# A projection group moved ahead of the gates of the last token chunk, and three exponentials moved ahead of a copy, in a two-layer mixer block

## The chip, the cores and the metric

The kernel runs on one core of one Trainium2 chip. The metric is device time in microseconds (us) of one execution. The kernel before takes 1721.24 us (median of 3 runs, 1720.3 to 1721.43). The trace is of one further execution of 1724.45 us, whose span is 1722.7 us.

## The reference, cut to what matters

The reference computes two layers over 256 context tokens and 1024 latent tokens of width 1024, all in float32. Layer 0 (gated linear attention and neighbourhood attention) ends in an output projection, a residual sum and a layer norm. Layer 1 begins with an mLSTM of four heads, whose queries, keys, values and gates are products of the normed and modulated tokens:

```python
qm, km, vm, _, gates = parts[:5]
q = heads(qm, ML_HEADS)
k = heads(km, ML_HEADS) * (ML_DQK ** -0.5)
v = heads(vm, ML_HEADS)
gp = gates.reshape(gates.shape[:2] + (2, 2, ML_HEADS)).astype(F32) + ml_gate_b.astype(F32)
...
x = layer_norm(ALPHA * x + gate[:, None] * y, ln_g[l], ln_b[l])
```

The mLSTM scan goes over chunks of 64 tokens in both directions. Its weights are exponentials of running sums and running maxima of the gates. Nothing of this is changed.

## The kernel before

**How the work is laid out.** Activations lie transposed, features on the 128 partitions, tokens along the free axis: `hT` (the input of the products) and `yT` each hold 8 tiles of 1280 tokens. A projection of 128 output features is a group of 8 matmuls per token chunk, one for each 128 input features, accumulated in one PSUM bank and then copied out. The token chunks are 0 to 256 (context), 256 to 768 and 768 to 1280. Values are made the other way round, tokens on the partitions, in groups of 256 tokens. The four mLSTM heads are handled as two pairs, called `("ml", 0, ...)` and `("ml", 1, ...)`. The two pairs' scans follow each other.

**Who does what in the stretch of the change.** `make_schedule` (L392) writes one list of steps by hand. Every engine walks through the same list in this order and issues only its own part of each step, so a step that waits holds up everything behind it on that engine, and on no other. The steps are:

- `("mm", kind, dest, t0, n, ...)`, in four parts, is one projection group. TensorE does its matmuls (L977). Its first part waits for the weight tile to have been loaded (L982) and for the PSUM bank to be free. At the fourth part ScalarE copies the bank out (L1737).
- `("scale", ...)` and `("next", ...)` end a layer norm. In `scale` VectorE multiplies (L1658) and ScalarE writes the modulated tokens to `hT` (L1908). In `next` VectorE makes the normed tokens in `yT` (L1676), and the DMA queue of SyncE (SP) stores them to HBM in pairs, after a wait for VectorE (L896 to L902). The last tokens (1024 to 1280) are normed last; this is norm 3.
- `gates` and `gates_sum` are the products for the gates of one chunk. `gates` (L1035) waits until the norms of its tokens are complete. ScalarE copies the result to a stage, TensorE sums it, and ScalarE writes two gate rows to `yT` (L1709, L1714).
- `("rows", 0)` (tokens 0 to 768) and `("rows", 1)` (768 to 1280) are the running sums and maxima over the gate rows, on VectorE (L1588). Each needs an exponential and a logarithm of ScalarE near its start (L1872, keys `rows_abs` and `rows_log`).
- `("rows_exp",)` is three exponentials on ScalarE over 64 x 1280 elements (L1879). They wait for the last VectorE operation of `rows`.
- `("rows_turn", t, ...)` transposes the rows of two token tiles on TensorE (L1282); the first one waits for the three exponentials (key `rows_act`). The scans follow.

**Pacing.** `pace` (L195) puts the steps of the norms and the products into one order. It counts planned microseconds of the norm steps, and it puts in products until their planned sum (tokens / 300 for each part of a projection) has caught up. What is left of the products comes behind the last norm step. The list called `ready` holds products of layer 1 that need only tokens 0 to 768; `rest` holds what needs the last tokens.

**Weights.** There are five tiles for weights (`WBUFS`), used in turn in the order of `PLAN`, which is the order in which the schedule first names each weight. SP issues the loads in its own walk through the schedule. It does so at the last product that uses a weight, and then loads up to four places further on:

```python
if s[0] == "mm" and LAST_PRODUCT.get(s[1]) == s:
    load_weights(WEIGHT_AT[s[1]] + WBUFS + (s[1][2:] == ("v0",)))
```

In `PLAN` the weights here stand as (out, 0, 7, 3), (ml, 0, q), (ml, 0, k), (ml, 0, v0), (ml, 0, v1), (ml, 1, q), (ml, 1, k). The last product with (ml, 0, q) is its group for tokens 768 to 1280, which stands in `rest`, behind `("rows", 0)`. So (ml, 1, q) is loaded when SP comes to that place. The tile that it is loaded into was last read by (out, 0, 7, 3), the last output projection.

Of the kernel before, what the change touches and what calls it, by code (L numbers as in the profile page):

```python
# [62 lines left out]
CHUNKS_LAT = CHUNKS_ALL[1:]  # L63
# [175 lines left out]
def project(kind, dest, chunks):  # L239

    out = []
    for t0, n in chunks:
        bank, stage = Slot(), Slot()
        out += [("mm", kind, dest, t0, n, bank, stage, part) for part in range(4)]
        if dest in ("rq", "kk") and t0 >= CTX:
            out.append(("rope", kind, dest, t0, n, Slot(), stage))
    if dest == "v":
        out += [("vgather", kind[1], g, Slot()) for g in range(-(-VG // 4))]
    return out
# [8 lines left out]
def values(group, j):  # L258

    return project((group, j, "v0"), "vt", [(t0, 2 * P) for t0 in range(0, T, 2 * P)])  # L260
# [40 lines left out]
def scans(l, fills):  # L301


    steps = [dict(l=l, p=p, i=i, t=(scan_order(0)[i], scan_order(1)[i]), wanted=(l == 0 or i >= CT))
             for p in range(2) for i in range(NT)]
    for q in steps:
        q["second"] = q["t"][0] in scan_order(1)[:q["i"]]
        assert q["second"] == (q["t"][1] in scan_order(0)[:q["i"]])
        q["d"] = (0, 1) if q["t"][0] < q["t"][1] else (1, 0)
        q["t"] = tuple(sorted(q["t"]))  # L310
    out, main = [], []
    for x in range(2 * NT + 3):
        if x in (NT, NT + 3):
            out += interleave(main, fills[x > NT])
            main = []
        now, one, two, three = (steps[x - y] if 0 <= x - y < 2 * NT else None for y in range(4))
        turned = three and three["second"] and three["wanted"]
        if turned:
            main.append(("lin_square", three))
        if two:  # L320
            main += [("lin_chunk", two, 0), ("lin_inside", two)]
        if one:
            main.append(("lin_attend", one))
        main.append(("gap",))
        if now:
            main.append(("lin_scale", now))
        if turned:
            main += [("lin_norm", three), ("lin_turn", three, Slot())]
        if two:
            main += [("lin_chunk", two, 1), ("lin_out", two)]  # L330
        if now:
            main.append(("lin_mul", now))
        main.append(("gap",))
    return out + interleave(main, fills[2])


def ada(l, tiles):

    out = []
    for x in range(0, len(tiles), 4):  # L340
        fs = tuple(tiles[x:x + 4])
        out += [("ada", l, fs, Slot()), ("ada_turn", l, fs, Slot())]
    return out


def ada_first(x):
    return (x, x + 1, 8 + x, 9 + x)
# [19 lines left out]
def qkv(group, j, chunks_q=CHUNKS_ALL):  # L367
    out = []
    for w in ("q", "k", "v") if group == "na" else ("q", "k"):
        out += project((group, j, w), w, chunks_q if w == "q" else CHUNKS_ALL)  # L370
    return out if group == "na" else out + values(group, j)


def between(products, extra):

    ends = [i + 1 for i, s in enumerate(products)
            if s[0] != "mm" and (i + 1 == len(products) or products[i + 1][0] == "mm")
            or s[0] == "mm" and s[7] == 3 and (i + 1 == len(products) or products[i + 1][0] == "mm")]
    out, at, used = [], 0, 0
    for n, e in enumerate(ends):  # L380
        out += products[at:e]
        at = e
        while used < (n + 1) * len(extra) // len(ends):
            out.append(extra[used])
            used += 1
    return out
# [5 lines left out]
def make_schedule():  # L392

    s, depth = [("setup",)], 0
    for x in range(0, KT, 2):
        s += [("ada", 0, ada_first(x), None), ("ada_turn", 0, ada_first(x), None), ("modulate", x), ("modulate", x + 1)]
        while depth < (x + 1 if x + 2 < KT else KT):
            s.append(("early", depth))
            depth += 1
    s += [("early_copy",)] + project(("lr",), "lr", CHUNKS_ALL)  # L400
    s += between(values("gla", 0), [("gate0", t) for t in GATE_ORDER])
    na = qkv("na", 0)
    na_v = [x for x in na if x[1] == ("na", 0, "v")]
    s += scans(0, [qkv("gla", 1), na_v, between([x for x in na if x not in na_v], ada(0, range(16, 24)))])
    gates = [project(("gate", 0, f), "gate", [c]) for f in range(8) for c in CHUNKS_ALL]
    fills = [between(qkv("na", j + 1), ada(1, range(8 * j, 8 * j + 8))) for j in range(3)] + [sum(gates[9:18], [])]
    s += attention(0, fills, [sum(gates[3 * j:3 * j + 3], []) for j in range(3)])
    s += sum(gates[18:], [])
    s += [("banks", 6)] + out_projection(0, 0, NORMS[:1])
    parts = [out_projection(0, ci, NORMS[ci:ci + 1]) for ci in range(1, 4)]  # L410
    s += [("blend",)] + pace(normalise(0, 0), parts[0])

    gates = [[(kind, t0, n, Slot(), stage) for kind in ("gates", "gates_sum")]
             for (t0, n), stage in ((c, Slot()) for c in CHUNKS_ALL)]
    q, k, v = project(("ml", 0, "q"), "q", CHUNKS_LAT), project(("ml", 0, "k"), "k", CHUNKS_ALL), values("ml", 0)
    ready = [gates[0][0], gates[1][0]] + q[:4] + [gates[0][1], gates[1][1]] + k[:8] + v[:12]
    rest = [gates[2][0], q[4], gates[2][1]] + q[5:] + [("rows", 1)] + k[8:] + v[12:] + [("rows_exp",)]
    s += pace(middle_norms(), parts[1] + parts[2] + ready) + [("rows", 0)] + rest
    q = project(("ml", 1, "q"), "q", CHUNKS_LAT)
    turns = [("rows_turn", t, Slot()) for t in range(0, NT, 2)]  # L420
    s += q[:4] + sum(([turn, x] for turn, x in zip(turns, q[4:])), []) + turns[4:]
    s += [("banks", 2)]
    fill = project(("ml", 1, "k"), "k", CHUNKS_ALL)
    fill += values("ml", 1)
    gates = [project(("gate", 1, f), "gate", [c]) for f in range(8) for c in CHUNKS_LAT]
    rq = [project(("sw", j, "q"), "rq", CHUNKS_LAT) for j in range(4)]
    s += scans(1, [fill + sum(gates[8:12], []), project(("sw", 0, "k"), "kk", CHUNKS_ALL) + gates[12],
                   project(("sw", 0, "v"), "vv", CHUNKS_ALL) + rq[0] + sum(gates[13:] + gates[:4], [])])
    s += attention(1, [rq[1], rq[2], rq[3], gates[7]], gates[4:7])
    s += [("banks", 6)] + out_projection(1, 1, NORMS[1:2])  # L430
    parts = [out_projection(1, ci, NORMS[ci:ci + 1]) for ci in range(2, 4)]
    s += pace(last_norms(), parts[0] + parts[1])
    s += [("column_sum", 1, 3)] + norm(1, 3)

    banks, stages, out = {}, {}, []
    single, newest, width = None, {}, 2
    for st in s:
        st = list(st)
        if st[0] == "one_bank":
            single = st[1] if st[2] else None  # L440
            if st[2]:
                BEFORE_ATT[st[1]] = newest[1]
            else:
                newest[1] = ("att", st[1])
            continue
        if st[0] == "banks":
            width = st[1]
            for b in range(2, 6):
                newest.pop(b, None)
                BANK_TURN.pop(b, None)  # L450
            continue
        at = {"mm": 5, "rope": 5, "ada": 3, "ada_turn": 3, "lin_turn": 2, "rows_turn": 2, "vgather": 3, "gates": 3, "gates_sum": 3}.get(st[0])
        if at is not None and st[at] is not None:
            fresh = st[at] not in banks
            st[at] = banks.setdefault(st[at], len(banks))
            if fresh:
                u = st[at]
                b = 0 if single is not None else min(range(width), key=lambda k: BANK_TURN.get(k, -1))
                BANK_OF[u], FORMER[u] = b, newest.get(b)
                newest[b], BANK_TURN[b] = u, u  # L460
        if st[0] in ("mm", "rope"):
            staged = st[2] == "gate" or (st[2] in ("rq", "kk") and st[3] >= CTX)
            st[6] = stages.setdefault(st[6], len(stages)) if staged else None
        if st[0] in ("gates", "gates_sum"):
            st[4] = stages.setdefault(st[4], len(stages))
        out.append(tuple(st))
    return out
# [1662 lines left out]
```

How the kernel before makes its waits and increments, by code:

```python
        def wait_bank(pe, u):  # L683
            former = FORMER[u]
            if former is None:
                return
            if isinstance(former, tuple):
                pe.wait_ge(*at(("softmax_dve", ("att", former[1], 3, N_UNITS[former[1]] - 1))))
            else:
                pe.wait_ge(*at(("proj_free", former)))
# [143 lines left out]
            def load_weights(upto):  # L835
                while sent[0] < min(upto, len(PLAN)):
                    n = sent[0]
                    if n >= WBUFS:
                        sp.wait_ge(*at(("weight_used", n - WBUFS)))
                    sp.dma_start(weights[:, n % WBUFS, :, :], a["weights"][n]).then_inc(
                        *up(f"weight_loaded{n % WBUFS}", ("weight", n), by=16))
                    sent[0] += 1
# [1 line left out]
            def load_residuals(upto, layer):  # L844
                while sent[1] < min(upto, len(RESID)) and RESID[sent[1]][1][1] == layer:
                    (_, l, f, _), t0, n, i = *RESID[sent[1]][1:2], *RESID[sent[1]][3:5], sent[1]
                    if i >= 4:
                        sp.wait_ge(*at(("resid_used", i - 4)))
                    if f == 0 and t0 == (CTX if l else 0):
                        sp.wait_ge(*at(("att_pe", l, 3)))
                        sp.wait_ge(*at(("y_turned", l, 7)))
                        if l:
                            for ci in range(1, 4):
                                sp.wait_ge(*at(("first_spill", ci)))
                                sp.wait_ge(*at(("spill", ci)))
```

## Time and profile before

| | |
|---|---|
| median of 3 runs | 1721.24 us |
| profiled execution | 1724.45 us, span 1722.7 us |
| TensorE (PE) busy | 1620.0 us, 94% |
| VectorE (DVE) busy | 672.9 us, 39% |
| ScalarE (ACT) busy | 548.4 us, 32% |
| GpSimd (POOL) busy | 36.6 us, 2% |
| mean granted TensorE clock | 0.983 of full speed |

Times of day in the rows are microseconds from the start of the span. L12 is line 12 of the kernel. One float32 matmul of 512 columns appears as two records, so a projection group of 8 matmuls counts x16. Most operations of ScalarE are issued through one helper and carry its line, L1701; they are told apart by the tiles that they write. The granted clock is 1.00 at 2.4 GHz and 0.50 at 1.2 GHz.

### The profile page before, as it was taken

The page shows a single profiled execution, that of the slowest core. Times are in us where ns is not written, and L with a number is a line of the kernel's source. Part 1 is how long each engine was busy: PE and PEld are TensorE (multiplying, and loading weights), DVE is VectorE, ACT ScalarE, POOL GpSimd, SP SyncE. Part 2 cuts the span into 40 slices and gives each one's busy share as a digit, 9 for nine tenths or more (in the row PEclk, how much of TensorE's full clock was granted, in tenths as well). Part 3 has the DMA queues.
Part 4 walks back from the last instruction along what each step waited for, and adds up shares of the span by engine and source line. Part 5 has one row for each costly group of instructions (what it writes and reads, how often), then busy time and mean ns, then how long its engine had stood idle before and what let it go on. Part 6 is the DMA issues. An engine that isn't in the chain of part 4 may idle for free.

```text
span 1722.7 us, 25991 instructions
## 1 busy us (share of the span) xinstructions
PE 1620.0 (94%) x10106; PEld 1023.8 (59%) x10106; DVE 672.9 (39%) x1537; ACT 548.4 (32%) x1253; POOL 36.6 (2%) x108
## 2 busy tenths in 40 slices
PE   6999999899999999888999989999899899999996
PEld 4676876556556556554746755675474355555475
DVE  2123443423313214321254735135345255555256
ACT  0242141323423324432121432124213355555024
POOL 0000000000000000000000000000000001111000
PEclk9999999899999999999999999999999899999999
DMA  9100021111223023000454511000001000000344
GB/s 381 58 25 25 2 99 63 62 62 59 89 74 123 16 70 123 25 13 14 149 181 153 178 45 49 25 26 26 13 2 50 13 13 14 25 13 14 128 140 160
DMA packets 41145, 120.63 MB, mean 70 GB/s; under 512 B 4288, under 2 KB 14784, under 8 KB 39744
## 3 DMA queue, kind: packets, MB, share of 16 engines
q1 hardware_dynamic: 41024, 118.97, 19.8%
q8 instruction: 82, 1.34, 0.3%
q14 instruction: 39, 0.32, 0.1%
HBM read 109.52 MB, written 9.44 MB: 69 GB/s over the span
## 4 chain that ended last, share of the span: by engine, by line
PE 77%; issue 16%; DVE 3%; ACT 3%; DMA 1%; POOL 0%; SPq 0%; DVEq 0%; ACTq 0%; POOLq 0%
PE proj L1012 22%; PE mixed L1012 15%; PE scores L1012 6%; PE proj L996 5%; PE mixed L996 4%; PE mixed L1132 3%; PE turned L1118 3%; PE scores L1230 2%; PE scores L1098 2%; PE scores L1258 2%; PE scores L1101 1%; ACT vstage L1701 1%; PE turned L1269 1%; PE mixed L957 1%; PE turned L957 1%
## 5 line engine op out<-in xcount | busy, mean ns | idle before, releaser
L1012 PE MATMUL proj<-hT,weights 128*128 128x512 f32 (+1 forms) x1264 | 513.5, 553 | 10.4 <-DVE yT L1380 3.6
L1012 PEld LDWEIGHTS proj<-hT,weights 128*128 128x128 f32 x1264 | 235.1, 194 | 215.8 <-issue 204.7
L1012 PE MATMUL mixed<-hT,weights 128*128 128x512 f32 (+1 forms) x336 | 144.5, 573 | 0.8 <-ACT pair L1701 0.8
L1012 PE MATMUL mixed<-yT,weights 128*128 128x256 f32 (+1 forms) x432 | 123.0, 442 | 0.0
L1701 ACT ACTIVATE work<-work,stat 128x640 f32<-128x640 f32 (+8 forms) x144 | 108.8, 755 | 42.8 <-DVE stat L1439 39.0
L1538 DVE SCALAR_TENSOR_TENSOR work<-work,turned 128x128 f32<-128x128 f32 (+1 forms) x152 | 53.1, 349 | 143.4 <-PE turned L1269 140.2
L1701 ACT ACTIVATE work<-turned 128x512 f32<-128x512 f32 (+2 forms) x136 | 72.7, 534 | 109.6 <-PE turned L1114 98.3
L1118 PEld LDWEIGHTS turned<-consts,work 128*128 128x128 f32 (+4 forms) x656 | 74.8, 140 | 54.6 <-issue 34.0
L1118 PE MATMUL turned<-consts,work 128*128 128x128 f32 (+4 forms) x656 | 99.8, 279 | 7.8 <-ACT work L1701 7.8
L1012 PEld LDWEIGHTS mixed<-yT,weights 128*128 128x128 f32 x432 | 82.1, 190 | 38.9 <-issue 31.1
L1012 PEld LDWEIGHTS mixed<-hT,weights 128*128 128x128 f32 x336 | 62.2, 191 | 62.3 <-issue 60.1
L1456 DVE COPY work<-turned 128x512 f32<-128x512 f32 (+1 forms) x72 | 46.6, 647 | 120.2 <-PE turned L1118 114.1
L1012 PE MATMUL scores<-yT,weights 128*128 128x256 f32 (+1 forms) x320 | 91.2, 443 | 0.0
L1701 ACT ACTIVATE work<-mixed 128x256 f32<-128x256 f32 x80 | 30.7, 383 | 176.7 <-PE mixed L1170 172.1
L996 PE MATMUL proj<-weights,hT 128*128 128x256 f32 x352 | 80.2, 382 | 0.0
L1012 PEld LDWEIGHTS scores<-yT,weights 128*128 128x128 f32 x320 | 60.8, 190 | 29.2 <-issue 23.4
L1701 ACT ACTIVATE vstage<-proj 128x512 f32<-128x512 f32 (+1 forms) x41 | 23.0, 560 | 164.9 <-PE proj L1012 142.6
L996 PEld LDWEIGHTS proj<-weights,hT 128*128 128x128 f32 x352 | 66.0, 190 | 11.5 <-issue 2.8
L1380 DVE TENSOR_TENSOR yT<-yT,proj 128x512 f32<-128x512 f32 (+1 forms) x28 | 17.4, 621 | 139.5 <-ACT vstage L1701 139.4
L996 PE MATMUL mixed<-weights,hT 128*128 128x256 f32 x288 | 65.1, 382 | 0.0
L996 PEld LDWEIGHTS mixed<-weights,hT 128*128 128x128 f32 x288 | 54.1, 190 | 9.7 <-issue 2.6
L1701 ACT ACTIVATE pair<-proj 128x512 f32<-128x512 f32 (+1 forms) x30 | 16.0, 533 | 123.0 <-PE proj L1012 100.8
(252 smaller groups left out, 2124.3 us busy)
## 6 DMA issues: line engine op xcount, KB each, us to landing
weights<-in_weights SPq DMA_DIRECT2D x138, 512.0 KB, 3.7
tables<-in_bias SPq DMA_DIRECT2D x8, 1281.0 KB, 7.2
hT<-in_xT SPq DMA_DIRECT2D x8, 640.0 KB, 16.0
yT<-in_weights SPq DMA_DIRECT2D x8, 512.0 KB, 8.4
work<-in_xT SPq DMA_DIRECT2D x24, 128.0 KB, 3.4
x1T<-yT SPq DMA_DIRECT2D x12, 256.0 KB, 2.2
work<-in_weights SPq DMA_DIRECT2D x4, 512.0 KB, 17.0
pair<-in_weights SPq DMA_DIRECT2D x4, 512.0 KB, 17.8
```

Source lines behind the costliest of these rows:

```text
L957: last = nc.tensor.matmul(early_bank(w, t0), weights[:, n, k, :], hT[:, k, t0:t0 + m], start=(k == 0 and (w == "q" or t0 > 0)), stop=(k == ...
L996: last = nc.tensor.matmul(PJ[BANK_OF[u]][:, 2 * x * P:2 * (x + 1) * P], tokens, weights[:, lo:hi + 1:hi - lo, k, :], start=(k == 0), stop= ...
L1012: last = nc.tensor.matmul(PJ[BANK_OF[u]][:, 0:n], weights[:, w % WBUFS, k, :], src[:, k, t0:t0 + n], start=(k == 0), stop=(k == KT - 1))
L1098: last = nc.tensor.matmul(to[:, lat_lo:lat_lo + unit.nk], q, unit_keys(keys, unit), start=True, stop=True)
L1118: last = nc.tensor.transpose(to[0:w, :], prob[uid[3] % 2][hh][:, o:o + w], ident)
L1132: last = nc.tensor.matmul(OV[rows, 0:P], vals[0:w, place, rows], prob_t[i % 2][0:w, at_col:at_col + P], start=(x == 0), stop=(x == nch - 1))
L1230: last = nc.tensor.matmul(out_of(l, h, x)[r, :], buf(q, "at")[r, o:o + CHUNK], pv(lin_slot(l, p))[r, t, h, 0:VW if l else P], start=False, ...
L1258: last = nc.tensor.matmul(out_of(l, h, x)[half * CHUNK:(half + 1) * CHUNK, :], buf(q, "qin")[r, o:o + CHUNK], state[d][r, 0:vw], start=(n ...
L1380: link(V.tensor_tensor(y, y, ps, ALU.mult), ("proj_free", u))
L1456: link(V.tensor_copy(prob_t[i % 2][:, 512 * g:512 * g + n], TP[1][:, 0:n]), ("pt", uid, g))
L1538: link(V.scalar_tensor_tensor(out=state[d][:, 0:vw], in0=state[d][:, 0:vw], scalar=decays(q)[:, o:o + 1], in1=TP[half][:, P:P + vw], op0=A ...
L1701: link(nc.scalar.activation(out, in_, func, **kw), *keys)
```

## The change

The group of the second pair's queries for tokens 256 to 768 (`others[:4]`) is appended to `ready`. It stood behind `rest` before, just ahead of the first `rows_turn`. It now stands ahead of the last chunk's `gates`. `("rows_exp",)` stood behind all of the value groups of the first pair. It now stands ahead of the last of them (tokens 1024 to 1280). No instruction is added or removed.

```diff
     ready = [gates[0][0], gates[1][0]] + q[:4] + [gates[0][1], gates[1][1]] + k[:8] + v[:12]
-    rest = [gates[2][0], q[4], gates[2][1]] + q[5:] + [("rows", 1)] + k[8:] + v[12:] + [("rows_exp",)]
+    others = project(("ml", 1, "q"), "q", CHUNKS_LAT)
+    ready += others[:4]
+    rest = [gates[2][0], q[4], gates[2][1]] + q[5:] + [("rows", 1)] + k[8:] + v[12:16] + [("rows_exp",)] + v[16:]
     s += pace(middle_norms(), parts[1] + parts[2] + ready) + [("rows", 0)] + rest
-    q = project(("ml", 1, "q"), "q", CHUNKS_LAT)
     turns = [("rows_turn", t, Slot()) for t in range(0, NT, 2)]
-    s += q[:4] + sum(([turn, x] for turn, x in zip(turns, q[4:])), []) + turns[4:]
+    s += sum(([turn, x] for turn, x in zip(turns, others[4:])), []) + turns[4:]
     s += [("banks", 2)]
```

## Rows read from the trace of the kernel before

**Rows 1.** The page, chain that ended last: shares of the span by engine.

```profile
PE 77%; issue 16%; DVE 3%; ACT 3%; DMA 1%; POOL 0%; SPq 0%; DVEq 0%; ACTq 0%; POOLq 0%
```

**Rows 2.** Windows: length, busy us (x instructions) by engine, clock, DMA share, GB/s.

```profile
1020.00:1026.00 6.00, 1.23 (x6) 0.75 (x4) 4.60 (x12) 4.44 (x8) 0.00 (x0) 0.97 0.14 49
1026.00:1040.00 14.00, 12.75 (x36) 4.87 (x37) 10.57 (x15) 4.99 (x8) 0.00 (x0) 0.77 0.28 92
```

**Rows 3.** Chain of waits, 1015 to 1080 us: start, length, what.

```profile
1017.78 3.47 PE proj L996 x16
...
1027.25 3.64 PE scores L1043 x16
...
1033.61 0.86 PE mixed L1051 x2
1034.47 5.15 PE scores L1012 x12
1039.62 6.87 PE mixed L1012 x16
...
1053.39 6.91 PE proj L996 x32
1060.30 6.87 PE scores L1012 x16
1067.16 0.52 PE scores L1288 x6
```

**Rows 4.** Timeline, TensorE: start, length, engine, line, operation [idle before, releaser].

```profile
979.05 1.92 PE L1043 MATMUL mixed<-hT,tables 128*32 128x512 f32 x16
```

**Rows 5.** Timeline of SP's DMA queue, 1027 to 1029 us.

```profile
1027.54 0.36 SPq L900 DMA_DIRECT2D x1T<-yT  x1
1027.95 0.47 SPq L840 DMA_DIRECT2D weights<-in_weights  x1
```

**Rows 6.** Line L840, the weight loads: that at 1027.95; then all from 950 to 1100.

```profile
DMA to landing us min/median/max: 3.7/3.7/3.7
...
DMA to landing us min/median/max: 3.4/3.7/6.5
```

**Rows 7.** Timeline, ScalarE, 1000 to 1100 us.

```profile
1028.92 0.84 ACT L1701 ACTIVATE yT<-yT 64x768 f32<-64x768 f32 x1 [1.92 <-DVE yT L1600]
1029.80 0.93 ACT L1701 ACTIVATE yT<-yT,cols 64x768 f32<-64x768 f32 x1
...
1039.71 0.60 ACT L1701 ACTIVATE pair<-scores 128x512 f32<-128x512 f32 x1 [3.76 <-PE scores L1012]
...
1061.02 1.27 ACT L1701 ACTIVATE work<-work 64x1280 f32<-64x1280 f32 x1
1062.33 2.57 ACT L1701 ACTIVATE yT<-yT 64x1280 f32<-64x1280 f32 x2
```

**Rows 8.** Timeline, VectorE, 1000 to 1100 us.

```profile
1030.84 0.95 DVE L1603 SCALAR_TENSOR_TENSOR yT<-yT 64x768 f32<-64x768 f32 x1 [2.01 <-ACT yT L1701]
...
1039.07 0.68 DVE L1600 SCALAR_TENSOR_TENSOR yT<-yT 64x512 f32<-64x512 f32 x1
1041.83 0.68 DVE L1603 SCALAR_TENSOR_TENSOR yT<-yT 64x512 f32<-64x512 f32 x1 [2.08 <-ACT yT L1701]
...
1055.02 3.00 DVE L1634 TENSOR_TENSOR yT<-yT,work 32x1280 f32<-32x1280 f32 x2
```

**Rows 9.** Windows of 1 us, columns as in Rows 2.

```profile
1025.00:1026.00 1.00, 0.00 (x0) 0.00 (x0) 0.58 (x2) 0.93 (x3) 0.00 (x0) 0.82 0.50 168
...
1032.00:1033.00 1.00, 1.00 (x3) 0.37 (x2) 0.83 (x3) 0.00 (x0) 0.00 (x0) 0.77 0.00 0
```

**Rows 10.** Timeline, TensorE, 1330 to 1375 us, after stalls elsewhere.

```profile
1330.20 1.96 PE L1012 MATMUL proj<-hT,weights 128*128 128x512 f32 x4 [1.62 <-DVE yT L1374]
...
1342.70 5.37 PE L1012 MATMUL proj<-hT,weights 128*128 128x512 f32 x8 [2.07 <-DVE yT L1380]
...
1349.66 3.70 PE L1012 MATMUL proj<-hT,weights 128*128 128x512 f32 x8
1357.03 1.12 PE L1279 MATMUL mixed<-consts,work 128*128 128x128 f32 x4 [3.67 <-DVE work L1586]
1358.71 9.52 PE L1012 MATMUL proj<-hT,weights 128*128 128x512 f32 x16
```

## Prediction

> **What bounds the kernel now.** I read the chain of waits first. It runs through TensorE for 77% of the span [rows 1], so what counts is when TensorE stands still, at which clock it runs, and what it waits for. Windows come next. In the stretch of the change TensorE is busy 1.23 of 6 us, and the clock is 0.77 of full over the 14 us behind that [rows 2]. The chain then shows the pieces: the value group of `ready` ends at 1017.78 + 3.47 = 1021.25; the gates of the last chunk start at 1027.25, when norm 3 has filled `hT`; so 6.0 us stand idle [rows 3]. The clock fell to 0.50 (1.2 GHz) at about 1025.64 (0.82 in a window of 1 us is 0.64 us at 1.00 and 0.36 at 0.50) and came back at about 1032.46 [rows 9]. TensorE worked 1032.46 - 1027.25 = 5.2 us at half speed and lost 2.6 us by it. A check: the gates took 3.64 us, against 1.92 for the same form at full clock [rows 3, 4]. The hole thus costs 6.0 + 2.6 = 8.6 us. From 1034.47 TensorE is unbroken up to the first `rows_turn` at 1067.16 [rows 3]. Last I read the queues of the other engines, because a moved step moves in each of them.
>
> **The change, part by part.**
>
> *The moved group itself.* It is 6.87 us of matmuls at full clock (the group at 1060.30) [rows 3]. It needs only tokens that are ready, so on its own it would fill the hole of 6.0 us. Its PSUM bank is no matter: by the turn order its former user is the gate sum of tokens 256 to 768, long copied out.
>
> *Its weight.* It needs the tile (ml, 1, q). SP issues that load at the last product with (ml, 0, q), which stays in `rest`. On SP's walk all stores of norm 3 lie ahead of it, and each waits for VectorE. The trace shows just that: the last store goes out at 1027.54, and the next entry of the queue is this load, at 1027.95 [rows 5]. The tile has long been free, for the last output projection was over before the gates at 979.05 [rows 4]; it is SP's order that holds the load. The change moves the use ahead of the hole, and not the load. The load takes 3.7 us to land, 3.4 to 6.5 for all loads around [rows 6]. The chain to `hT` and the stores (norm 3 on ScalarE and VectorE) waits for nothing that is moved, so the load still goes out at 1027.95 and lands at 1031.65 (1031.35 to 1034.45). There is no way round for TensorE: the gates, ready at 1027.25, are queued behind the waiting group. The idle time grows from 6.0 to 1031.65 - 1021.25 = 10.4 us.
>
> The Trainium skill, "DMA: Bandwidth & Descriptors", section "Rules for kernel authors", says to issue a DMA early, compute, and wait on its semaphore late. This change puts the wait some 39 us earlier (1060.30 to 1021.25) with the issue where it was, so the rule speaks against it. The same page's fixed cost of about 2.0 us plus bytes over 436 GB/s (section "Anatomy of one DMA", which is for another issuing path) gives an estimate of 3.2 us for 512 KB; the trace has 3.7, and by the page the time would be 0.5 us less.
>
> *The clock.* Between 1021.25 and 1031.65 it falls as before, and TensorE again works a while at half speed after it resumes. The nearest row is 5.2 us, a loss of 2.6. The bounds come from other stalls: behind one of 2.07 us eight records took 5.37 where they take 3.70, a loss of 1.7; behind one of 3.67 us a group of 16 records took 9.52 where 6.87 is usual in the chain, and the transposes ahead of it 1.12, half of it lost: about 2.6 + 0.6 = 3.2 [rows 3, 10]. I take 2.6, as now, with 1.7 and 3.2 as ends. So the moved group ends at 1031.65 + 6.87 + 2.6 = 1041.12.
>
> *What is queued behind it on ScalarE.* `pace` decides where its copy stands. At the `rstd` of norm 3 the planned products are at 85.92 and the norms at 86.2, and each part adds 512 / 300 = 1.71. So the four parts fall behind `rstd`, `scale` 2, `scale` 5 and `next` 0. ScalarE's copy belongs to the fourth part, thus behind all eight `scale` steps: `hT` is not held up. But it stands ahead of `("rows", 0)`. ScalarE's exponential and logarithm, which ran from 1028.92 to 1030.73 [rows 7], now wait for the copy (0.60, as the one at 1039.71): 1041.15 + 0.60 + 0.03 + 1.81 = 1043.59. VectorE waits for them, and its first L1603 moves from 1030.84 [rows 8] to 1043.7, by 12.86 us.
>
> *The rows chain.* From there to the second L1600, which ended at 1039.75, nothing changes but the shift. The second pair of exponential and logarithm lost 0.56 us behind the copy at 1039.71 [rows 7, 8]; now VectorE is the late one and this goes. So the chain ends at 1058.02 - 0.56 + 12.86 = 1070.32 (1058.02 is the end of L1634 [rows 8]).
>
> *The moved exponentials.* They took 1061.02 to 1064.90, 3.88 us, and started behind the copy of the last values, 3.0 us after VectorE was done [rows 7, 8]. Ahead of that copy they start with VectorE: 1070.4 + 3.88 = 1074.28. The copy goes behind them. The scan needs it only with its values, so it costs nothing; if it did, 0.6 us.
>
> *TensorE in the meantime.* After 1041.12: gates 1.92, the first part of the queries 1.72 (a quarter of 6.87), the gate sum 0.86, which needs the stage at about 1044.25 and finds it there; then 5.15 + 6.87 + 2 x 6.91 [rows 3, 4]. That is 1071.5. The first `rows_turn` waits for the exponentials until 1074.35: a new stall of 2.9 us, where before the moved group covered them. `rows_turn` thus comes 1074.35 - 1067.16 = 7.2 us later than now.
>
> *The second fall of the clock.* A stall of 1.62 us left the records at 1.96 for four, the full speed; those of 2.07 and 3.67 us did not [rows 10]. A stall of 2.9 us lies between the two latter, so I take the smaller loss, 1.7 us (0 to 3.2). The Trainium skill, "TensorE: Matmul & The Clock Gate", section "What's actually happening", says that the point of change depends on a phase that runs free of the kernel. By it the loss here may also be nothing, which is the second rival.
>
> *Sum.* 7.2 + 1.7 = 8.9 us. Behind the turns the same work follows at the same distance, and all engines are shifted alike, so nothing gives it back. The terms are of the execution of 1724.45 us; its stretch is taken as that of the runs, and 1721.24 + 8.9 = 1730.2 us.
>
> **The rivals.**
>
> *Faster: the weight is there in time.* If the load were out by about 1017.6, the moved group would run from 1021.25 to 1028.12 at full clock. The gates would start 0.9 us later than now, with no loss by the clock. The sum would end at 1028.12 + 1.92 + 1.72 + 0.86 = 1032.62, and the last values at 1058.5. The rows chain would end at 1058.02 - 0.56 = 1057.46 and the exponentials at 1061.4, so the turn comes 5.7 us earlier: -5.7, or -4.0 if the clock falls in that stall too: 1717.2, or 1715.5. For it: the tile is free since before 979.05. Against it: SP's order [rows 5], in which no load stands ahead of the stores. It decides at the issue time of this one load: each us later than 1017.6 is an us lost. 0.05.
>
> *The clock stays up in the new stall.* Then 1721.24 + 7.2 = 1728.4. For it: a stall of 1.62 us cost nothing. Against: 2.07 us did. 0.25.
>
> *Only the wait for the weight counts.* If the rows were ready by the time TensorE comes, the turn would be at 1071.5: +4.3, 1725.5. It needs ScalarE not to hold the rows behind the copy; its one queue says otherwise. 0.06.
>
> *A slower load.* The stores just ahead of it could hold it up. At 6.5 us [rows 6] both chains slip by 2.8: 1733.0. For it: one of the loads around took as long; against: this very one, behind the same stores, took 3.7. 0.06.
>
> **How the numbers follow.** The forecast, slower by 8.9, has 0.58. Range: 1726.5 to 1733.5. It takes in the second rival, the bounds 1.7 and 3.2 on the first clock loss, and most of the fourth; it leaves out the faster case and most of the third. Differences within 0.2% (3.4 us) can't be told from none. Faster by more: 0.05. Within: 0.03, from the third rival with a short clock loss. Slower by more: 0.92.
>
> **What would show it.** Right: TensorE's longest wait in the stretch is one for a weight DMA of about 10.4 us, and behind it come the queries, not the gates; SP issues the load at about 1027.95; ScalarE's first exponential over 64 x 768 starts at about 1041.8; VectorE waits some 15 us in L1603 of part 0; and the first `rows_turn` stands idle about 3 us for ScalarE, at 1074. Wrong: a weight load ahead of the last store; or a `rows_turn` that doesn't wait, which would refute the rows chain as the second limit.

## The result, and the profile after

The changed kernel takes 1732.61 us (median of 4 runs, 1732.13 to 1734.23) against 1721.12 us for the kernel before (median of 4, 1720.3 to 1721.43). The ratio is 1.0071, with a 95% interval of 1.0056 to 1.0086: 0.7% slower. Measured again (e11) it was 1730.68 against 1720.9 us, ratio 1.0060 (1.0046 to 1.0073). The profiled execution took 1732.67 us, with a span of 1730.9 us.

The page after, busy time by engine and the chain's shares (the row of before is in [rows 1]):

```profile
PE 1620.8 (94%) x10106; PEld 1022.4 (59%) x10106; DVE 672.9 (39%) x1537; ACT 549.4 (32%) x1253; POOL 36.8 (2%) x108
PE 75%; issue 16%; DVE 4%; ACT 3%; DMA 1%; POOL 0%; SPq 0%; DVEq 0%; ACTq 0%; POOLq 0%
```

The page barely shows the loss. TensorE's timeline does (start, length, operation, in brackets the idle time before and what ended it):

```profile
1014.34 3.62 PE L997 MATMUL proj<-weights,hT 128*128 128x256 f32 x16
1028.39 9.90 PE L1013 MATMUL scores<-hT,weights 128*128 128x512 f32 x16 [10.44 <-DMA weights<-in_weights]
1038.23 1.92 PE L1044 MATMUL scores<-hT,tables 128*32 128x512 f32 x16
...
1061.68 7.07 PE L997 MATMUL scores<-weights,hT 128*128 128x256 f32 x32
1071.63 0.90 PE L1289 MATMUL scores<-consts,yT 64*128 64x64 f32 x6 [2.87 <-ACT yT L1702]
1072.46 3.21 PE L1013 MATMUL mixed<-hT,weights 128*128 128x512 f32 x4
1075.60 0.59 PE L1289 MATMUL mixed<-consts,yT 64*128 64x64 f32 x6
1076.12 1.98 PE L1013 MATMUL mixed<-hT,weights 128*128 128x512 f32 x4
```

The hole of 6.0 us ahead of the gates [rows 2, 3] is now one of 10.44 us ahead of the moved queries, and what ends it is the weight. The gates behind them run at full speed, 1.92 us as in [rows 4]. TensorE then stands idle for 2.87 us ahead of the first `rows_turn`, and the piece behind it takes 3.21 us where the next one of its kind takes 1.98. SP's queue answers to [rows 5]; the chain of waits gives the landing:

```profile
1020.47 4.16 SPq L901 DMA_DIRECT2D x1T<-yT  x4
1024.67 0.47 SPq L841 DMA_DIRECT2D weights<-in_weights  x1
```

```profile
1024.67 3.68 DMA weights<-in_weights
1028.39 9.92 PE scores L1013 x16
1038.38 0.61 ACT pair L1702
1039.01 0.85 ACT yT L1702
```

The load still goes out behind the four stores and lands 3.7 us later. (This trace is 3.28 us ahead of that of before when the last value group ends, 1017.96 against 1021.24, so its 1024.67 is the 1027.95 of [rows 5].) The chain then shows the second limit: behind the queries comes ScalarE's copy, and only behind it the exponential of `rows`. ScalarE's own timeline and then VectorE's, for [rows 7, 8]:

```profile
1038.38 0.60 ACT L1702 ACTIVATE pair<-scores 128x512 f32<-128x512 f32 x1 [14.66 <-PE scores L1013]
1039.01 0.84 ACT L1702 ACTIVATE yT<-yT 64x768 f32<-64x768 f32 x1
...
1067.70 1.27 ACT L1702 ACTIVATE work<-work 64x1280 f32<-64x1280 f32 x1 [5.15 <-DVE yT L1635]
1069.00 2.57 ACT L1702 ACTIVATE yT<-yT 64x1280 f32<-64x1280 f32 x2
```

```profile
1040.94 0.95 DVE L1604 SCALAR_TENSOR_TENSOR yT<-yT 64x768 f32<-64x768 f32 x1 [15.39 <-ACT yT L1702]
...
1064.61 3.00 DVE L1635 TENSOR_TENSOR yT<-yT,work 32x1280 f32<-32x1280 f32 x2
```

The clock in windows (columns as in [rows 2]), for [rows 9]: at half for the whole 5.6 us after TensorE resumes, and again for 3.4 us behind the second stall.

```profile
1028.40:1034.00 5.60, 5.60 (x7) 2.50 (x8) 0.00 (x0) 0.00 (x0) 0.00 (x0) 0.50 0.00 0
1071.60:1075.00 3.40, 3.37 (x9) 1.89 (x10) 0.00 (x0) 0.81 (x2) 0.00 (x0) 0.51 0.40 163
```

**Three stretches.** The time varies by some us between executions of one kernel, so all traces are cut in three for comparison. The *start* goes to the end of the last value group ahead of the hole. The *stretch* goes from there to the start of the last `rows_turn`. The *rest* follows. "Clock" is half of TensorE's busy time at 1.2 GHz, summed over windows of 0.25 us; "net" is the stretch less its clock. Time against before is the difference of the medians of runs taken together. The lengths of the stretch are good to 0.2 us, all in the same direction, so their differences are good to 0.1.

| kernel | stretch | its clock | net | rest | its clock | time against before |
|---|---|---|---|---|---|---|
| before | 55.7 | 2.6 | 53.1 | 645.9 | 9.3 | |
| changed | 65.1 | 4.5 | 60.6 | 648.0 | 11.3 | +11.5 |
| changed again (e11) | 65.6 | 5.2 | 60.4 | 646.1 | 9.5 | +9.8 |
| e1, early load | 51.7 | 1.7 | 50.0 | 646.2 | 9.6 | -0.4 |
| e8, e1 again | 51.7 | 1.7 | 50.0 | 646.1 | 9.6 | -2.2 |
| e2, queries only | 66.7 | 4.3 | 62.4 | 644.6 | 8.1 | +13.2 |
| e3, exponentials only | 55.8 | 2.7 | 53.1 | 645.8 | 9.3 | +0.3 |
| e4, rows first | 61.8 | 2.1 | 59.7 | 646.3 | 9.7 | +9.6 |
| e5, load after first store | 62.3 | 5.2 | 57.0 | 646.2 | 9.5 | +8.6 |
| e6, early load in before | 54.9 | 1.7 | 53.2 | 644.3 | 7.8 | -0.1 |
| e7, early load and cover | 45.9 | 0.0 | 45.9 | 647.4 | 11.1 | -9.7 |
| e9, late load and cover | 59.1 | 2.5 | 56.7 | 646.3 | 9.8 | +2.7 |
| e10, e7 with old exponentials | 45.9 | 0.0 | 45.9 | 645.0 | 8.3 | -10.5 |

From before to changed: the net stretch grew by 7.5 (10.44 - 6.02 = 4.4 at the DMA, 2.9 at `rows_turn`, and 0.2 that no row names), its clock by 1.9, and the rest by 2.1, of which 2.0 is clock. That is 11.5 us, as much as the medians differ by. The same sum with the second trace of the changed kernel (e11) gives 10.1 against a measured 9.8. The match to a tenth is luck in part, since these sums leave out the start: its end lies anywhere from 1016.1 to 1021.2 us in the 13 traces, though the products up to there are the same. The spans differ by 8.2 only, because the profiled execution of before took 3.3 us more in the start; it was 3.2 us above its median.

### The profile page after: what moved, and what is told of

It reads as the page before. It is cut to its first block, busy times and chain, and to the rows that moved or that the text cites. A ratio compares the mean times of both kernels' runs of the same rounds, so it can differ in the third digit from the quotient of the medians.

```text
span 1730.9 us, 25991 instructions
## 1 busy us (share of the span) xinstructions
PE 1620.8 (94%) x10106; PEld 1022.4 (59%) x10106; DVE 672.9 (39%) x1537; ACT 549.4 (32%) x1253; POOL 36.8 (2%) x108
## 4 chain that ended last, share of the span: by engine, by line
PE 75%; issue 16%; DVE 4%; ACT 3%; DMA 1%; POOL 0%; SPq 0%; DVEq 0%; ACTq 0%; POOLq 0%
PE proj L1013 22%; PE mixed L1013 15%; PE scores L1013 6%; PE proj L997 4%; PE mixed L997 3%; PE mixed L1133 3%; PE turned L1119 3%; PE scores L1231 2%; PE scores L1099 2%; PE scores L1259 2%; PE scores L1102 1%; ACT vstage L1702 1%; PE turned L1270 1%; PE mixed L958 1%; PE turned L958 1%
## 5 line engine op out<-in xcount | busy, mean ns | idle before, releaser
L1013 PE MATMUL proj<-hT,weights 128*128 128x512 f32 (+1 forms) x1264 | 512.4, 552 | 10.4 <-DVE yT L1381 3.6
L1013 PE MATMUL mixed<-hT,weights 128*128 128x512 f32 (+1 forms) x352 | 155.0, 585 | 0.8 <-ACT pair L1702 0.8
L1539 DVE SCALAR_TENSOR_TENSOR work<-work,turned 128x128 f32<-128x128 f32 (+1 forms) x152 | 53.1, 349 | 142.4 <-PE turned L1270 139.2
L1013 PEld LDWEIGHTS mixed<-hT,weights 128*128 128x128 f32 x352 | 66.3, 195 | 68.4 <-issue 66.2
L997 PE MATMUL mixed<-weights,hT 128*128 128x256 f32 x256 | 58.0, 382 | 0.0
L997 PEld LDWEIGHTS mixed<-weights,hT 128*128 128x128 f32 x256 | 48.0, 190 | 8.5 <-issue 2.1
```

Of the source, the lines that this page charges most:

```text
L997: last = nc.tensor.matmul(PJ[BANK_OF[u]][:, 2 * x * P:2 * (x + 1) * P], tokens, weights[:, lo:hi + 1:hi - lo, k, :], start=(k == 0), stop= ...
L1013: last = nc.tensor.matmul(PJ[BANK_OF[u]][:, 0:n], weights[:, w % WBUFS, k, :], src[:, k, t0:t0 + n], start=(k == 0), stop=(k == KT - 1))
L1539: link(V.scalar_tensor_tensor(out=state[d][:, 0:vw], in0=state[d][:, 0:vw], scalar=decays(q)[:, o:o + 1], in1=TP[half][:, P:P + vw], op0=A ...
```

## The experiments

**e1: the load in time.** The changed kernel, with SP's load ahead of the stores of norm 3:

```diff
+                if s[0] == "next" and s[1:] == (3, 1):
+                    load_weights(WEIGHT_AT[("ml", 1, "q")] + 1)
                 if s[0] == "next" and s[2] % 2:
```

> The changed kernel, with one load moved in SP's walk: the tile (ml, 1, q) is loaded ahead of the first store of norm 3, where its buffer has long been free. Theory (the late load is the cause): TensorE no longer waits for a weight DMA, the moved group fills the hole, ScalarE's first exponential over 64 x 768 starts near its old place, and the first rows_turn still waits about 2.9 us for the moved exponentials. Against before: -4.0 if the clock falls in that stall, -5.7 if not, so 1715.5 to 1717.2 us; against the changed kernel -15 to -17. Rival (the order of the products costs by itself, through the rows chain or ScalarE's queue): the wait for the DMA goes but the time stays above that of before, 1722 or more.

Measured: 1719.31 us (11 runs, 1715.85 to 1720.99) against 1719.68, ratio 0.9994 (0.9985 to 1.0004). The timeline of TensorE:

```profile
1014.34 3.62 PE L999 MATMUL proj<-weights,hT 128*128 128x256 f32 x16
1017.79 7.03 PE L1015 MATMUL scores<-hT,weights 128*128 128x512 f32 x16
1024.75 1.92 PE L1046 MATMUL scores<-hT,tables 128*32 128x512 f32 x16
...
1058.26 0.58 PE L1291 MATMUL scores<-consts,yT 64*128 64x64 f32 x6 [2.98 <-ACT yT L1704]
1058.77 2.66 PE L1015 MATMUL mixed<-hT,weights 128*128 128x512 f32 x4
```

SP's queue and VectorE's timeline in the same trace:

```profile
987.13 0.49 SPq L841 DMA_DIRECT2D weights<-in_weights  x1
```

```profile
1027.56 0.95 DVE L1606 SCALAR_TENSOR_TENSOR yT<-yT 64x768 f32<-64x768 f32 x1 [2.01 <-ACT yT L1704]
```

The load goes out 30.7 us ahead of its use. The hole and its low clock are gone, and nothing else was altered: the late load is the cause of the first loss. VectorE waits 2.01 us in part 0 of `rows`, as in before [rows 8], and not 15.39. The stall at `rows_turn` is there all the same, 2.98 us, so it doesn't need a late copy on ScalarE: the moved group no longer stands ahead of the turns to cover it. The stretch is 4.0 us shorter than in before, as expected. The time is not: it is 0.4 us below before, where 4.0 to 5.7 were expected.

**e8: the same kernel again.**

> The same kernel as e1_early_load, for a second trace and more timed runs. There the trace had the turn 5.7 us earlier than in before, and a low clock of 3.4 us behind the new stall, which makes -4.0; the median was only 0.4 us below before. Theory A (the loss of clock behind the new stall is 1.7 in some executions and 3.4 in others, and later falls come with it): in this trace the first rows_turn again waits 3.0 us and comes 40.2 us after the end of the last value group of the first stage; what differs from run to run is the time at the low clock only; median 1 to 4 us below before. Theory B (something else in the later stages is longer): the stretch behind the turns is over 658 us with no more low clock in it.

Measured: 1717.47 us (11 runs, 1710.92 to 1721.62) against 1719.67, ratio 0.9987 (0.9975 to 0.9998). The stretch is again 51.7 us, and the rest 646.1 with 9.6 of clock, so theory B holds in neither trace. The two medians lie 0.4 and 2.2 us below before; the stretch says 4.0. The 1.8 to 3.6 us between them aren't in either trace, and both traced executions (1717.49 and 1715.94 us) were faster than the median of their kernel, by 1.8 and 1.5 us. The mean granted clock of the 22 timed runs is no higher than that of before (0.984 for both), although in the traces the stretch spends 3.4 us at the low clock against 6.8 in before, which would be 0.001 more. That hints at the clock at other stalls. It isn't shown: the other timed runs have no trace, and theory B isn't excluded for them.

**e5: a dose.** The load behind the first of the four stores (`(3, 3)` in place of `(3, 1)` in the edit of e1).

> A dose of the delay: the changed kernel with the load of (ml, 1, q) behind the first of the four stores of norm 3, not behind the last. In the changed kernel's trace the first store goes out at 1020.5 and the load at 1024.7, so the load goes out about 3.8 us earlier. Theory (TensorE and, through ScalarE's queue, the rows chain both hang on the landing): the wait for the DMA is about 6.6 in place of 10.4 us, the first rows_turn comes 3.8 us earlier, and the time is 3.8 us below the changed kernel's, give or take 1.7 of the clock: about 12.3 - 0.8 - 3.8 = 7.5 us above before, 1727 us. Rival (a fixed harm of having the group there): about as slow as the changed kernel, above 1730.

Measured: 1728.28 us (5 runs, 1727.76 to 1728.71) against 1719.67, ratio 1.0055 (1.0041 to 1.0069). SP's queue and TensorE:

```profile
1020.77 0.36 SPq L903 DMA_DIRECT2D x1T<-yT  x1
1021.17 0.47 SPq L841 DMA_DIRECT2D weights<-in_weights  x1
1022.04 2.89 SPq L903 DMA_DIRECT2D x1T<-yT  x3
```

```profile
1025.24 9.27 PE L1015 MATMUL scores<-hT,weights 128*128 128x512 f32 x16 [6.98 <-DMA weights<-in_weights]
...
1067.84 0.90 PE L1291 MATMUL scores<-consts,yT 64*128 64x64 f32 x6 [2.87 <-ACT yT L1704]
1068.67 3.78 PE L1015 MATMUL mixed<-hT,weights 128*128 128x512 f32 x4
```

The wait is 3.46 us shorter (3.8 were expected; this load took 4.0 us to land), the net stretch 3.6, and the stall at `rows_turn` is the same to 0.01 us. So both engines' chains hang on the landing. The whole stretch fell by 2.8 only, since the clock took 3.0 behind `rows_turn` here, and 1.6 in the changed kernel's first trace; against its second (e11), with 3.0 as here, it fell by 3.3. The time, 8.6 us above before where about 7.5 was expected, is 1.2 to 2.9 us below the changed kernel's +9.8 and +11.5. Timed runs don't show more of where the rest went.

**e6: the early load in the kernel before.** The edit of e1 on before.

> A control: the kernel before with only the load of (ml, 1, q) moved ahead of the stores of norm 3. Theory: in the kernel before the tile is used at about 1060 us and lands at 1031 us, so an earlier load changes nothing: the same time as before within 0.1%. Rival (the early load helps or harms by itself, beside the stores of norm 2 or by freeing the queue behind the stores of norm 3): a difference of over 2 us.

Measured: 1719.57 us (11 runs) against 1719.67, ratio 1.0001 (0.9993 to 1.001). The load by itself does nothing.

**e2 and e3: each part alone.** e2 leaves the exponentials where they were; e3 moves them alone.

```diff
-    rest = ... + v[12:16] + [("rows_exp",)] + v[16:]
+    rest = ... + v[12:] + [("rows_exp",)]
```

> The first part of the change alone: the query group ahead of the gates, the three exponentials behind the copy of the last values, as in the kernel before. Theory: the exponentials start 0.6 us behind the end of the last values instead of as soon as VectorE is done; the copy ends about 2 us after that point, so rows_turn waits about 4.5 us in place of 2.9 and the time is 1.5 to 2 us above the changed kernel: about 1734.3 us. Rival (the moved exponentials are part of the harm): below the changed kernel, 1731 or less.

> The second part of the change alone, on the kernel before: only the three exponentials ahead of the copy of the last values. Theory: they start at VectorE's end, 3.0 us earlier, but rows_turn comes behind the query group anyway, so nothing changes: 1721.2 us within 0.1%. Rival (the delayed copy of the last values or the earlier exponentials count by themselves): a difference of over 2 us either way.

Measured: e2 1732.88 us (6 runs, 1729.23 to 1735.48) against 1719.68, ratio 1.0072 (1.0056 to 1.0088); e3 1719.96 us (12 runs), ratio 1.0000 (0.999 to 1.0011). In e2's trace `rows_turn` waits 1.8 us longer than in the changed kernel, by the net stretch (62.4 against 60.6):

```profile
1071.08 0.90 PE L1289 MATMUL scores<-consts,yT 64*128 64x64 f32 x6 [4.65 <-ACT yT L1702]
```

e2 is no faster than the changed kernel, and e3 is as fast as before: the queries do all the harm. The moved exponentials give back 1.8 us of it in the traces (the medians don't resolve that), and alone they are worth nothing.

**e4: rows ahead of the copy.** The moved group one step later, behind `("rows", 0)`:

```diff
-    s += pace(middle_norms(), parts[1] + parts[2] + ready) + [("rows", 0)] + rest
+    s += pace(middle_norms(), parts[1] + parts[2] + ready) + [("rows", 0)] + others[:4] + rest
```

> The changed kernel with the moved group one step later: behind rows 0, still ahead of the last chunk's gates. TensorE's order is the same and the load is as late, so it waits 10.4 us as before; but ScalarE's exponential and logarithm for rows 0 now stand ahead of the copy of the moved group. Theory (two limits, the second being ScalarE's queue behind the copy): VectorE's wait in rows 0 goes back to about 2 us, the first rows_turn doesn't wait, and of the 11.4 us lost only the part of the longer DMA wait remains: 10.4 - 6.0 = 4.4, so about 1725.5 us (1724 to 1728 with the clock's phase). Rival (only the DMA wait and the clock count, the stall at rows_turn is a by-product): no gain over the changed kernel, 1731 to 1734.

Measured: 1729.29 us (5 runs, 1728.07 to 1730.7) against 1719.68, ratio 1.0053 (1.0038 to 1.0069). The expectation, 1724 to 1728, failed, and the rival's 1731 to 1734 as well. VectorE's timeline has the reason:

```profile
1027.90 0.95 DVE L1603 SCALAR_TENSOR_TENSOR yT<-yT 64x768 f32<-64x768 f32 x1 [2.01 <-ACT yT L1701]
...
1044.26 0.68 DVE L1600 SCALAR_TENSOR_TENSOR yT<-yT 64x512 f32<-64x512 f32 x1 [8.16 <-ACT yT L1701]
1050.04 0.68 DVE L1603 SCALAR_TENSOR_TENSOR yT<-yT 64x512 f32<-64x512 f32 x1 [5.11 <-ACT yT L1701]
```

The wait in part 0 went back to 2.0 us, as meant. But part 1 needs the gate rows of the last chunk, which come late because TensorE is late, and its exponential then stands behind the copy of the next query group. The 13.4 us won in part 0 were mostly lost again in part 1, where VectorE waits 8.2 + 5.1 us against 1.6 in the changed kernel, and `rows_turn` still waited 1.73 us. The rows hang on TensorE's delay at two places, not at one.

**e9: the second limit taken away.** The late load kept; the other half of the queries as one group ahead of the row transposes:

```diff
-    s += sum(([turn, x] for turn, x in zip(turns, others[4:])), []) + turns[4:]
+    s += others[4:] + turns
```

> The changed kernel with the load as late as it is there, but the other half of the moved queries as one group ahead of the five row transposes. It takes away the second limit alone (the rows chain behind ScalarE's copy, which reached rows_turn 2.9 us late), since 6.9 us of products now cover it. Theory (two limits in series): TensorE still waits 10.4 us for the DMA, and the first rows_turn doesn't wait. From the end of the last stalled products: 3.2 us less for the stall, 1.7 for the clock and 0.8 to 1 for the unsplit parts, so 5 to 6 us below the changed kernel, about 1726 us. Rival (the stall at rows_turn is not a cost of its own): within 2 us of the changed kernel.

Measured: 1723.62 us (11 runs, 1721.27 to 1727.74) against 1720.9, ratio 1.0015 (1.0006 to 1.0024), and 7.1 us below the changed kernel measured beside it (e11), where 5 to 6 were expected:

```profile
1028.04 9.58 PE L1013 MATMUL scores<-hT,weights 128*128 128x512 f32 x16 [10.57 <-DMA weights<-in_weights]
...
1067.91 7.03 PE L1013 MATMUL scores<-hT,weights 128*128 128x512 f32 x16
1074.88 1.34 PE L1289 MATMUL mixed<-consts,yT 64*128 64x64 f32 x18
```

There is no wait at `rows_turn`. So the stall there, with its clock and the split parts, was worth 6 us (65.1 to 59.1 in the traces; 6.5 from e11's 65.6).

**e7 and e10: both mended.** The edits of e1 and e9 together; e10 also puts the exponentials back.

> The changed kernel with the early load of e1_early_load and, beside it, the second half of the moved queries (tokens 768 to 1280) as one whole group ahead of the five row transposes, which then come back to back. Theory: the group (6.9 us) covers the 3.0 us in which rows_turn waited for the exponentials in e1_early_load, so TensorE doesn't stand still from the last values to the scans, and the clock has no cause to fall there. From the chain: the stall of 3.0, the clock's 1.7 and about 0.8 of start-up between the split parts go, 5.5 us less than e1_early_load; 8.5 to 9.4 us below before if all of it shows in the time, 1710 to 1711.5 us. Rival (the clock's low stretches come back at other stalls, so that a stall taken away gives less than its length): 3 to 6 us below before, 1713.5 to 1716.5.

> e7_cover with the three exponentials behind the copy of the last values, as in the kernel before: it asks what the second part of the change is worth once the rest is mended. Theory: they end at about 2.4 us before the first rows_turn (the copy ends at 1054.1 on e7_cover's clock, the exponentials at 1058.0, the turn comes at 1060.5), so the time is that of e7_cover within 0.1%, 1710 us. Rival (the earlier exponentials are needed): 1 to 3 us above e7_cover.

Measured: e7 1709.95 us (5 runs, 1707.89 to 1712.63) against 1719.67, ratio 0.9950 (0.9938 to 0.9962); e10 1710.39 us (5 runs) against 1720.9, ratio 0.9939 (0.9927 to 0.9951). Both beat the two kernels. TensorE in e7:

```profile
1016.19 7.03 PE L1015 MATMUL scores<-hT,weights 128*128 128x512 f32 x16
1023.15 1.92 PE L1046 MATMUL scores<-hT,tables 128*32 128x512 f32 x16
...
1053.51 7.03 PE L1015 MATMUL scores<-hT,weights 128*128 128x512 f32 x16
1060.47 1.34 PE L1291 MATMUL mixed<-consts,yT 64*128 64x64 f32 x18
```

TensorE doesn't stand still from the values to the scans. The whole 9.8 us of the stretch show in the time here, slightly more than the 8.5 to 9.4 expected of e7, so its rival (3 to 6 us) is out. The second part of the change is worth nothing in this form either.

**e11: the changed kernel again.**

> The changed kernel again, on the chip and beside the kernel before of this call, for a second trace. Theory: TensorE waits about 10.4 us for the weight DMA and 2.9 us at the first rows_turn, as in the first trace; from the end of the last value group ahead of the hole to the last rows_turn 65 us against 55.7 in before, give or take 1.7 of the clock; 9 to 12 us above before.

Measured: 1730.68 us (5 runs, 1729.37 to 1732.14), with waits of 10.34 and 2.87 us. What differs from the first trace is the clock: 2.2 us in place of 2.9 behind the first stall, 9.5 in place of 11.3 in the rest, and 3.0 in place of 1.6 behind the second stall, where TensorE's timeline reads:

```profile
1069.06 0.90 PE L1289 MATMUL scores<-consts,yT 64*128 64x64 f32 x6 [2.87 <-ACT yT L1702]
1069.89 3.78 PE L1013 MATMUL mixed<-hT,weights 128*128 128x512 f32 x4
1073.60 0.90 PE L1289 MATMUL mixed<-consts,yT 64*128 64x64 f32 x6
1074.43 2.33 PE L1013 MATMUL mixed<-hT,weights 128*128 128x512 f32 x4
```

## Why the prediction was right

**The weight's wait.** Forecast 10.4 us, measured 10.44, and ended by the DMA; the load went out right behind the last store, at 1027.95 on the clock of before's trace as forecast, and landed in 3.68 us against 3.7. Shown by e1 (without it the hole is gone), e5 (3.46 us less of it, 3.6 less in the stretch) and e6 (alone it is nothing). The Trainium skill's rule ("DMA: Bandwidth & Descriptors", "Rules for kernel authors": issue early, wait late) is what the change broke and e1 restores. The estimate of 3.2 us for the load, from the same page (section "Anatomy of one DMA", for loads issued by GpSimd), is 0.5 short of the measured 3.68.

**ScalarE's queue and the rows.** Forecast: VectorE waits some 15 us in `rows`, and the first `rows_turn` 2.9 us. Measured 15.39 and 2.87. That this stall is a limit of its own is shown by e9. The third rival (only the wait for the weight counts) is refuted by the changed kernel's trace. The forecast's reason against it, one queue on ScalarE, was only part of it. e4 took the copy out of the way of the first part of the rows, and the second part was late all the same. And e1, with the copy in time, has the same stall of 2.98 us. In the changed kernel the copy ties the rows to the landing, so that both chains slip together; the stall itself comes from the cover that the moved group took away.

**The exponentials.** Forecast: they start with VectorE and cost nothing beside. They started 0.09 us after it (1067.61, 1067.70). e3 shows that alone they are worth nothing, e2 that they save 1.8 us of the stall which the first part made.

**The clock.** Forecast 2.6 us behind the first stall, as before, and 1.7 behind the second, 8.9 in all for the stretch. In the trace they are 2.9 and 1.6, and the stretch is 9.4 longer. The second rival, that the clock stays up in the stall, didn't happen in any trace of the six with a stall of 2.87 us or more at that place: losses of 1.6, 1.7, 1.7, 2.1, 3.0 and 3.0 us. With e4's 1.73 us it stayed up.

**What was off in size.** The forecast was +8.9 (with which the sum gives 1730.1, not 1730.2), the median +11.5, and +9.8 in the second measurement. Of this the stretch is 9.4 and 9.9 in the traces, 0.5 to 1.0 over the forecast, by the clock behind the two stalls (4.5 and 5.2 us against 4.3) and by the 0.2 that no row names. The larger mis-sized step is the sentence that all behind the turns follows at the same distance. The work does: less its clock, the rest is 636.2 to 636.7 us in all 13 traces. The clock in it doesn't: it costs 7.8 to 11.3 us, and in the changed kernel's trace it costs 2.0 more than in before's. As the second trace (e11) had 9.5, this part varies from execution to execution, and no trace ties it to the change. Whether the mean over many runs grows with a stall more is open, as with e1 and e8: the first four timed runs of the changed kernel all had a granted clock of 0.979 or 0.980, the five of e11 0.979 to 0.982.

## What to carry to other kernels

Products that are moved ahead to fill a hole bring their weight's load along only if the queue that issues it is moved too: look up in the trace where the load goes out, and behind what. Follow the moved step in every engine's order, since its copy was what held up the next chain here. Products are cover in the place that they leave as well; give that place another cover before they go (e7, -9.7 us; without it e1 had -0.4 and -2.2).

## What the runs showed of the hardware

A stall of the same length costs a different time from one execution to the next: 2.87 us ahead of the same instructions took 1.6 us of clock in one trace of the changed kernel and 3.0 in the other (e11), and the same rest 7.8 to 11.3. These figures agree with the Trainium skill, "TensorE: Matmul & The Clock Gate", section "What's actually happening", by which the point of change depends on a phase free of the kernel. For the reader this means that one trace's clock is one draw: compare stretches with the low clock taken off, which agreed to 0.5 us in 636.
